# Sample's latent scores: from fp32 products to three passes of split operands

## What is computed

```
q_lat = jnp.einsum('bqhd,chd->bqhc', q_nope, w_uk)
s = (jnp.einsum('bqhc,bkc->bhqk', q_lat, ckv)
     + jnp.einsum('bqhr,bkr->bhqk', q_pe, kpe)).astype(jnp.float32) * ATTN_SCALE
p = jax.nn.softmax(jnp.where(mask[None, None], s, -jnp.inf), axis=-1).astype(ckv.dtype)
o_lat = jnp.einsum('bqhk,bkc->bqhc', p, ckv)
```

## Time and profile before

| | us |
|---|---|
| median of 3 runs (lowest, highest) | 802.34 (802.24, 803.27) |
| profiled execution | 802.13 |
| its span | 800.3 |
| TensorE busy | 789.0 |
| DVE, ACT, POOL busy | 588.0, 479.4, 95.7 |

### The profile page before, as it was taken

The page is one execution under the profiler, slowest core; times in us unless marked ns, Lnnn a source line. Parts: engine busy times, 40 slices in busy tenths (PEclk is TensorE's granted clock), DMA queues, the critical chain, the costliest instruction groups (busy, mean ns, idle before and its releaser), DMA issues.

```text
span 800.3 us, 15387 instructions
## 1 busy us (share of the span) xinstructions
PE 789.0 (99%) x6179; PEld 761.0 (95%) x6179; DVE 588.0 (73%) x971; ACT 479.4 (60%) x840; POOL 95.7 (12%) x196
## 2 busy tenths in 40 slices
PE   9999999999999999999999999999999999999995
PEld 7999999999899899999999999999999999999994
DVE  5898946846855868988989897875698887655452
ACT  5793854855655578666575664444548887633432
POOL 0225112022013001111000100000000000001212
PEclk9999999999999999999999999999999999999997
DMA  8559356246346335555456544655445555554531
GB/s 310 166 178 365 109 159 212 81 158 196 113 127 189 135 116 177 157 182 159 146 175 177 176 146 137 225 158 167 160 158 171 162 158 164 174 165 158 164 127 59
DMA packets 37559, 132.38 MB, mean 165 GB/s; under 512 B 4768, under 2 KB 5424, under 8 KB 37232
## 3 DMA queue, kind: packets, MB, share of 16 engines
q1 hardware_dynamic: 30960, 109.49, 43.0%
q0 software_dynamic: 5760, 20.06, 7.8%
q10 hardware_dynamic: 768, 1.84, 0.6%
HBM read 127.17 MB, written 4.08 MB: 164 GB/s over the span
## 4 chain that ended last, share of the span: by engine, by line
PE 98%; ACT 1%; DVE 1%; DMA 0%; issue 0%; ACTq 0%; DVEq 0%
PE ps_acc L447 19%; PE ps_acc L448 18%; PE ps_acc L449 18%; PE ps_row L448 3%; PE ps_row L447 3%; PE ps_row L449 3%; PE ps_tr L447 2%; PE ps_tr L448 2%; PE ps_cb L448 2%; PE ps_tr L449 2%; PE ps_cb L449 2%; PE ps_cb L447 2%; PE ps_row L771 1%; PE ps_acc L571 1%; PE ps_tr L739 1%; PE ps_ss L633 1%
## 5 line engine op out<-in xcount | busy, mean ns | idle before, releaser
L1346 DVE TENSOR_TENSOR wlo<-wraw,whi 128x1024 fp32r<-128x1024 f32 x203 | 247.5, 1225 | 133.8 <-ACT whi L941 133.2
L941 ACT CAST whi<-wraw 128x1024 fp32r<-128x1024 f32 x203 | 212.1, 1046 | 134.3 <-DMA wraw<-in_wst 133.8
L447 PE MATMUL ps_acc<-xh,whi 128*128 128x288 f32 x560 | 171.0, 305 | 0.0
L448 PE MATMUL ps_acc<-xl,whi 128*128 128x288 f32 x560 | 165.2, 295 | 0.0
L449 PE MATMUL ps_acc<-xh,wlo 128*128 128x288 f32 x560 | 165.1, 295 | 0.0
L447 PEld LDWEIGHTS ps_acc<-xh,whi 128*128 128x128 f32 x560 | 105.3, 188 | 7.7 <-issue 6.9
L448 PEld LDWEIGHTS ps_acc<-xl,whi 128*128 128x128 f32 x560 | 105.4, 188 | 0.5
L449 PEld LDWEIGHTS ps_acc<-xh,wlo 128*128 128x128 f32 x560 | 105.3, 188 | 0.0
L1401 DVE SCALAR_TENSOR_TENSOR cv<-xp,vec,cv 128x292 f32<-128x292 f32 x96 | 50.1, 522 | 16.2 <-ACT cv L1003 13.8
L447 PE MATMUL ps_acc<-o_h,whi 128*128 128x288 f32 x128 | 39.1, 306 | 0.0
L448 PE MATMUL ps_acc<-o_l,whi 128*128 128x288 f32 x128 | 37.8, 295 | 0.0
(11 more groups left out here) (461 smaller groups left out, 2290.6 us busy)
## 6 DMA issues: line engine op xcount, KB each, us to landing
wraw<-in_wst SPq DMA_DIRECT2D x203, 512.0 KB, 3.6
rows<-rows_p POOLq DMA_DIRECT2D x8, 512.0 KB, 4.6
v_raw<-in_wst POOLq DMA_DIRECT2D x8, 512.0 KB, 6.1
side<-in_ukT POOLq DMA_DIRECT2D x8, 256.0 KB, 3.9
side_v<-in_ukT POOLq DMA_DIRECT2D x8, 256.0 KB, 3.8
out_ssm<-s_out POOLq DMA_DIRECT2D x8, 256.0 KB, 2.5
x<-in_xT ACTq DMA_DIRECT2D x4, 288.0 KB, 4.9
ax<-in_xT POOLq DMA_DIRECT2D x1, 1152.0 KB, 6.1
```

The costliest lines, as they stand in the source:

```text
L447: pe.matmul(out, w, mh, start=first, stop=False)
L448: pe.matmul(out, w, ml, start=False, stop=False)
L941: act.copy(whi[:, s % RING, :], wraw[:, s % RING, :]).then_inc(split_hi, 1)
L1346: tt(wlo[:, s % RING, :], wraw[:, s % RING, :], whi[:, s % RING, :].bitcast(F32), ALU.subtract).then_inc(split_lo, 1)
```

## The change

The sample's latent scores are now made of three fp32r passes per product, 24 in a round.
- The cache is split once, in round 0. ACT, after the second `k_copy` and ahead of `fill_in(0)`, waits for `cache_in` 32 (both cache DMAs) and for POOL's copy of the new rows, and casts four blocks of 544 columns to `ckvT_h`; DVE, after the weight part that follows `qnat_copy`, subtracts four times (`cache_low`) into `ckvT_l`, which lies on `ckvT` itself.
- The queries are split in each round: `qlat_copy` makes a high part by a copy out of PSUM, waits for it, and subtracts it from PSUM into a low part. The scores wait for both.
- Space: three blocks of `ckvT_h` lie in the part of `xc` that is written only in round 3, the fourth lies where `rows` is; `ssT` shares its place with the low queries. So `decay_rows(0)` moves from ahead of round 0 into round 3, behind the scores of that round.
- Some semaphores are joined (`ckt_cp` into `kab_done`, `pick_made` into `ln_cm`).

```
         ckvT = after("ckvT", [P, RB, KEYS])
+        ckvT_l = at("ckvT_l", [P, RB, KEYS], end[0] - RB * KEYS * 4, F32R)
...
-        qlat = after("qlat", [P, RB, P])
+        qlat_h = after("qlat_h", [P, RB, P], F32R)
...
-        ssT = after("ssT", [P, 5, P])
+        qlat_l = after("qlat_l", [P, RB, P], F32R)
+        ssT = at("ssT", [P, 5, P], end[0] - RB * P * 4)
...
+        ckvT_h3 = at("ckvT_h3", [P, 1, KEYS], end[0] - HPG * SEQ * 4, F32R)
+        ckvT_h0 = at("ckvT_h0", [P, 3, KEYS], Z_XC + (fill(ROUNDS - 1, 0) * CW * 4 + 31) // 32 * 32, F32R)
...
             def sample_scores(i):
-                pe.wait_ge(qlat_cp, i + 1)
+                pe.wait_ge(qlat_cp, 2 * i + 2)
                 pe.wait_ge(qz_twice, 16 * i + 16)
                 pe.wait_ge(cache_in, 32)
                 pe.wait_ge(kall_in, 32)
-                pe.wait_ge(ckt_cp, 1)
+                pe.wait_ge(cache_lo, RB)
...
                     for c in range(RB):
-                        pe.matmul(bank[:, 0:half], qlat[:, c, :], ckvT[:, c, keys], start=c == 0, stop=False)
+                        passes(bank[:, 0:half], qlat_h[:, c, :], qlat_l[:, c, :], ckvT_h(c)[:, keys],
+                               ckvT_l[:, c, keys], c == 0, False)
...
                 for c in range(2):
                     ahead(("k", i, c))
                     k_copy(i, c)
+                if i == 0:
+                    act.wait_ge(cache_in, 32)
+                    act.wait_ge(kab_done, 9)
+                    for c in range(RB):
+                        act.copy(ckvT_h(c), ckvT[:, c, :]).then_inc(cache_hi, 1)
                 fill_in(0)
...
             def qlat_copy(i):
                 dve.wait_ge(qlat_done, i + 1)
-                dve.tensor_copy(qlat[:].rearrange("p c q -> p (c q)"), ps_ss[:]).then_inc(qlat_cp, 1)
+                high = qlat_h[:].rearrange("p c q -> p (c q)")
+                dve.tensor_copy(high, ps_ss[:]).then_inc(qlat_cp, 1)
+                dve.wait_ge(qlat_cp, 2 * i + 1)
+                tt(qlat_l[:].rearrange("p c q -> p (c q)"), ps_ss[:], high.bitcast(F32), ALU.subtract
+                   ).then_inc(qlat_cp, 1)
+
+            def cache_low():
+                for c in range(RB):
+                    dve.wait_ge(cache_hi, c + 1)
+                    tt(ckvT_l[:, c, :], ckvT[:, c, :], ckvT_h(c).bitcast(F32), ALU.subtract).then_inc(cache_lo, 1)
...
                 qnat_copy(i)
                 ahead(("k", i, 1))
+                if i == 0:
+                    cache_low()
                 ahead(("x", fill(i, 0)))
                 qlat_copy(i)
...
             pool.dma_start(ckvK[:, 0:4, :], cacheK).then_inc(cache_in, 16)
-            decay_rows(0)
...
+                    if j == 2 and i == ROUNDS - 1:
+                        pool.wait_ge(ssc_done, ROUNDS)
+                        decay_rows(0)
                     conv(fill(i, j))
```

More of the change, by code:

```diff
@@ L262, in layer_program, with ckvT_h @@
         rows = after("rows", [P, HPG, SEQ])
+        ckvT_h3 = at("ckvT_h3", [P, 1, KEYS], end[0] - HPG * SEQ * 4, F32R)
+        ckvT_h0 = at("ckvT_h0", [P, 3, KEYS], Z_XC + (fill(ROUNDS - 1, 0) * CW * 4 + 31) // 32 * 32, F32R)
+        assert end[0] <= Z_XC + CB * CW * 4
+        def ckvT_h(c):
+            return ckvT_h0[:, c, :] if c < 3 else ckvT_h3[:, 0, :]
         o_h = at("o_h", [P, HEADS, T], Z_A, F32R)
@@ L347, in layer_program @@
             "lat_sq", "lat_sum", "lat_std", "lat_rec", "lat_n", "lat_hi", "lat_lo")
-        ckv_out, conv_out, ck_pe, ck_cp, ckt_cp, cache_in, kall_in = sems(
-            "ckv_out", "conv_out", "ck_pe", "ck_cp", "ckt_cp", "cache_in", "kall_in")
+        ckv_out, conv_out, ck_pe, ck_cp, cache_hi, cache_lo, cache_in, kall_in = sems(
+            "ckv_out", "conv_out", "ck_pe", "ck_cp", "cache_hi", "cache_lo", "cache_in", "kall_in")
         half_done, rope_m, rope_done, qz_ready, qz_twice, qnat_done, qnat_cp, qlat_done, qlat_cp = sems(
@@ L366, in layer_program @@
             "mix_g", "mix_t", "mix_hi", "mix_lo", "ax_in", "ax_done")
[L367 to L368 removed]
+        ln_run, ln_sq, ln_pe, ln_cm, ln_xb, ln_step, ln_std, ln_w0, ln_w, ln_z = sems(
+            "ln_run", "ln_sq", "ln_pe", "ln_cm", "ln_xb", "ln_step", "ln_std", "ln_w0", "ln_w", "ln_z")
         gb_hi, gb_lo, e_hi, e_lo, u_step, u_evac, d_evac, ah_step, ah_done = sems(
@@ L877, in last_sums @@
                 quarter_sums(squares_q, sq2[:, 7, :], True).then_inc(ln_pe, 1)
-                pe.wait_ge(pick_made, 1)
+                pe.wait_ge(ln_cm, 3)
                 pe.wait_ge(ln_step, 2)
@@ L1917, in _ @@
             dve.tensor_copy(pick[:], ident.rearrange("p (q c) -> p q c", q=4)[:, :, 0:1].to_broadcast([P, 4, P])
-                            ).then_inc(pick_made, 1)
+                            ).then_inc(ln_cm, 1)
             dve.wait_ge(ah_done, KB)
@@ L1992, in _ @@
             pool.wait_ge(kpe_out, 16)
-            pool.tensor_copy(ckvT[:, :, PAST:KEYS], ckvn[:, :, SEQ:T]).then_inc(ckt_cp, 1)
+            pool.tensor_copy(ckvT[:, :, PAST:KEYS], ckvn[:, :, SEQ:T]).then_inc(kab_done, 1)
             pool.wait_ge(lat_lo, 1)
@@ L2006, in side_v_load @@
                     pool.wait_ge(lat_lo, 2)
-                    pool.wait_ge(ckt_cp, 1)
+                    pool.wait_ge(kab_done, 9)
                     pool.wait_ge(ck_pe, 1)
```

## The result

The changed kernel takes **804.75 us** (median of 13 runs, 803.53 to 805.32), the kernel before it on the same chip 802.45 us (median of 13, 801.93 to 803.42). The ratio is 1.0027, with a 95% interval of 1.0019 to 1.0034: slower by about 2.3 us, where 804.5 was forecast. The profiled execution took 804.42 us, its span is 802.6; before, 802.13 and 800.3.

A forecast was written before the change was run, and what follows sets the result against it. TensorE, busy 99% of the span, was taken to bound the kernel: 802.13 + 4.2 (round 0) - 2.0 (rounds 1 to 3) = 804.3, plus 0.2 for the median of runs, 804.5 us; range 801.9 to 806.8.

The forecast's parts named there:

- Passes: Scores, all four rounds: 24 passes at 0.1247 us, 2.99 instead of 3.66 us, gaining 0.67 per round, 2.7 in all.
- Rounds 1 to 3: Low queries add about 0.75 us on DVE, hidden to within 0.05; these rounds gain 3 x 0.67 = 2.0 us.
- Landing: Round 0: ckvK, issued at 62.34, lands 12.9 us later, at 75.24; ACT's casts wait for it.
- rival A: Round 0: the cache lands earlier because rows no longer shares the engines; at 73.0 the time is 802.3 us; chance 0.30.
- ACT and DVE in round 0: Casts 0.64 us, subtractions 0.70 in DVE's idle time, low queries 0.68; first max step at 83.72, DVE 5.27 late.
- TensorE in round 0: Waits of 1.8 us before scores, 2.1 before the turn of the prompt's probabilities, 0.9 before latent outputs.
- 4.2 late: TensorE leaves round 0 4.2 us late at the latent outputs, that round's gain included.
- Moved work: Rows DMAs moved to round 3, low cache in place, shifted tiles, joined semaphores: cost nothing, at most a few tenths.
- B: Round 0: an early landing keeps DVE's delay below the latent outputs' slack and passes win, 799.6 us; chance 0.10.
- C: Round 0: the clock falls to 0.52 in a new TensorE wait, costing 1.1 to 2.7 us, 805.6 to 807.2; chance 0.08.
- it decides from 71.4: Round 0: the faster rival takes over when the cache lands at 71.4, where the time is 800.7 us.

The follow-up runs named there:

- k7: g4 with the low part of the queries subtracted twice in rounds 1 to 3; 800.76 us.
- g2: The kernel before with only the rows DMAs moved into round 3, behind its scores; 802.47 us.
- h6: The changed kernel, but round 0's casts and subtractions read the layer's input, so ACT doesn't wait for the cache landing; 800.83 us.
- g1: The changed kernel with ckvK counted on another semaphore, so scores and cache split wait for ckvT alone; 801.07 us.
- g4: The changed kernel with fp32 scores in round 0 and the cache split late in that round; passes only in rounds 1 to 3; 800.33 us.
- h5: g1 with ckvK issued only behind the value weights of round 0; 799.99 us.
- k9: The kernel before with ckvK issued behind the value weights of round 0, on the semaphore of the rotary keys; 802.51 us.
- g3: The kernel before with one wait added: ACT waits for both cache DMAs in round 0, no split, no passes; 804.41 us.

## Why the prediction was right

The forecast was 804.5 us, the result is 804.75; the profiled execution is 2.3 above the one before, where 2.2 was the sum. By its steps:

- **Passes.** 0.1247 us each was the middle of two bounds; measured 0.1245. By the estimate from the Trainium skill (TensorE: Matmul & The Clock Gate, Back-to-back issue gap), 0.116, a round would have gained 0.88 (3.66 less 24 x 0.116) and not the 0.68 measured. The trace does not agree for these passes. The section gives that formula for an isolated matmul, and says that in a stream of weight loads and matmuls, as here, both set the spacing. That the fp32 matmuls agree with it, as the prediction says, holds only if each of them, 0.229 us long, streams its 272 columns twice; no row shows that.
- **Rounds 1 to 3.** Forecast 3 x 0.67 = 2.0, measured 1.93 (0.56, 0.68 and 0.69). The subtraction was to be hidden to within 0.05: it took exactly the idle of the earlier trace rows and no more, and k7 shows that twice as much would still be hidden.
- **Landing.** Taken as 75.24, measured 74.86 (62.59 and 12.27). That it depends on nothing issued behind it was a choice against rival A; g2 bears it out.
- **ACT and DVE in round 0.** Casts 0.64 us against 0.644 measured, subtractions 0.70 against 0.718, low queries 0.68 against 0.69. First max step 83.72 against 83.30, so 4.85 late and not 5.27: 0.38 of the difference is the landing. (The 88.21 that the prediction reads as the end of the prompt's last scaling is the start of the instruction behind it; the scaling ended at 88.29, and nothing changes by it.) The subtractions lay in idle time, as forecast (h6).
- **TensorE in round 0.** The three waits stand where they were forecast and are released by what was named. Sizes: 1.8, 2.1 and 0.9 were forecast; by the view of the waits they are 1.0, 2.0 and 0.6, by starts 0.1 to 0.2 more. The sum of these was **4.2 late**; measured 3.76 against the kernel before, 3.5 without the 0.23 that was there before. This is the term that was mis-sized, by 0.7 us. The landing explains 0.6 of it: ckvK took 12.27 us from its issue where 12.9 was taken, so it came 0.38 earlier than assumed though it was issued 0.25 later.
- **Two small terms that the sum lacked** cancel that: the 0.23 before the round, and about 0.5 behind the rounds. In the out projection TensorE waited 0.61 us at 567.24, behind a weight DMA that took 4.20 us from 560.14. The kernel before has no such wait in its traced execution, but g1, g4, h5 and k9 show one of 0.2 to 0.5 us in the same place. k9 differs from the kernel before only in where one DMA of round 0 is issued and waited for. That it is scatter of a transfer and no effect of the change is likely from that, not shown. So the agreement within 0.25 us is in part luck, better than the sum deserves; about 0.7 would be fair.
- **Moved work.** Nothing was forecast. For the rows DMAs g2 measures nothing; the moved tiles and joined semaphores were not tried alone, but g4, which has them all, gains 2.2 us in three rounds where the passes are worth 2.0.

The rivals. **A** (the cache lands earlier when rows no longer share the engines): wrong, the landing is 12.5 and 12.9 us behind the issue with them and 11.5 to 14.4 without; 10.7 would have been needed for 73.0. **B** (the cover holds, 799.6): not what this change does, but its price was right. h5 realises it, with ckvT at 70.4, and takes 799.99; "it decides from 71.4" agrees, as g1's trace, with 72.4, is 1.8 us slower than h5's (801.67 and 799.91). **C** (the clock falls in the waits): the windows around the three waits (columns: stretch, length, busy us of PE, PEld, DVE, ACT and POOL, granted clock, DMA share, GB/s):

```profile
78.00:82.00 4.00, 3.03 (x24) 2.79 (x23) 3.89 (x7) 3.92 (x9) 1.21 (x3) 1.00 0.32 82
90.00:95.00 5.00, 3.00 (x26) 2.77 (x25) 4.38 (x15) 4.94 (x13) 0.21 (x1) 1.00 0.49 167
98.00:100.00 2.00, 1.39 (x12) 1.16 (x11) 1.72 (x5) 1.97 (x6) 0.31 (x2) 1.00 0.07 25
```

The granted clock is 1.00, the 2.4 GHz level, in all three. A wait of 2.0 us between dense passes did not lower it here.

Four expectations of the experiments missed their range. g1 and h6 were both to take 799.8 and took 801.07 and 800.83. Both had the wait for ckvK removed, and then met the next transfer: ckvT at 72.4 in g1, a weight chunk at 73.8 in h6. Each was seen in one traced execution; how their 1.0 to 1.3 us divide over the many executions stays open. g3 was to take 803.8, at most 804.2, and took 804.41; its traced execution, 803.52, is one of its faster ones, and what the slower ones did was not seen. k7 took 800.76, just above its 800.7.

## What to carry to other kernels

When a change lets an engine wait for a transfer, price it by the work that stands behind that wait on the same engine, not by what reads the data: here one semaphore shared by two DMAs cost 3.7 us, more than the shorter matmuls of all four rounds brought. Let each consumer wait for the transfer that it reads, issue first what is wanted first, and put one-off work ahead of a wait or into idle time that is already there. Where TensorE sets the time, a gain per round is only what is left after the one late chain of the first round, so follow that chain to the last TensorE instruction that waits on it, and take off the slack there (1.1 us here).

## What the runs showed of the hardware

- A split pass of 272 columns with a weight load of its own takes 0.1245 us, between 0.117 for 256 and 0.132 for 288. That is 8 to 10 ns above columns/2.4 + 2.5 ns, the gap that the Trainium skill (TensorE: Matmul & The Clock Gate, Back-to-back issue gap) gives for an isolated matmul, in all three shapes.
- Landings of the same 1 MB transfer scatter by 2 us and more. In the traced executions of the kernels that issue ckvK right behind ckvT, ckvT takes 8.1 (h6) to 10.8 us (g1) and ckvK 11.5 (k7) to 14.4 us (g4). The cast of the weight chunk that ACT takes next scatters too: in the traces in which it waits for its own transfer alone it starts between 71.8 (k9) and 74.3 us (g2). Whether a wait for such a landing widens the scatter of the times is not shown: g3 ranges over 3.45 us in 11 runs and g2, without the wait, over 0.70, but the kernel before ranges over 1.90 in 28 and the changed kernel, with the wait, over 1.79 in 13.
- ckvK issued at 73 us instead of 62 lands in 7.5 us (h5) and 9.2 (k9) instead of 11.5 to 14.4: the same megabyte. At 62 it is queued right behind ckvT, at 73 it isn't; how much of the difference is ckvT and how much the weights under way beside it was not separated.
